# Seven block products for the turned queries and keys, their weight sums on GpSimd, and an earlier first modulation sum

## The reference, cut to what matters

```python
mod = jax.nn.silu(cvec) @ w_mod_l + b_mod_l            # 6 rows of 1024
sh1, sc1, g1, sh2, sc2, g2 = jnp.split(mod, 6, axis=-1)
h = x * (1.0 + sc1) + sh1
qa, ka, va, qb, kb, vb, qc, kc, vc = jnp.split(h @ w_in_l, _in_offsets(), axis=-1)
...
ga, gb, gc = jnp.split(jax.nn.sigmoid(h @ w_gate_l + b_gate_l), N_BRANCH, axis=-1)
y = (ga * (oa @ w_br_l[0]) + gb * (ob @ w_br_l[1]) + gc * (oc @ w_br_l[2])) @ w_o_l
```

## Time and profile before

| | us |
|---|---|
| median of 3 runs | 2136.37 (2136.27 to 2140.67) |
| the profiled execution's own time | 2136.38 |
| its span in the profile | 2134.3 |
| PE busy | 2007.2, 94% |
| DVE busy | 1292.1, 61% |
| POOL busy | 238.2, 11% |

### The profile page before, as it was taken

How to read it: one execution, slowest core, us unless ns; L and a number is a source line. 1 busy time by engine, 2 the same in 40 slices (tenths; PEclk the granted TensorE clock), 3 DMA queues, 4 the chain that set the end, 5 groups by cost and what they waited for, 6 DMA issues and landing times. The chain is left out here.

```text
span 2134.3 us, 25339 instructions
## 1 busy us (share of the span) xinstructions
PE 2007.2 (94%) x9546; PEld 1173.9 (55%) x9546; DVE 1292.1 (61%) x2031; ACT 513.9 (24%) x1007; POOL 238.2 (11%) x250
## 2 busy tenths in 40 slices
PE   7999999999999999699899999999999999979995
PEld 3457766566467754344244676656755676434432
DVE  2747747675456665756444574776744665866664
ACT  2114401143124400122130342003402342002221
POOL 1000020421110000100120002031101000010003
PEclk9999999999999999899999999999999999989998
DMA  7631046411120061689781111552111105238996
GB/s 284 243 118 40 21 143 222 138 55 44 40 82 21 33 279 79 247 341 362 257 278 48 64 41 64 195 185 87 48 57 46 43 21 221 105 133 322 385 350 199
DMA packets 62682, 317.00 MB, mean 149 GB/s; under 512 B 14824, under 2 KB 15280, under 8 KB 34272
## 3 DMA queue, kind: packets, MB, share of 16 engines
q1 hardware_dynamic: 32688, 232.41, 28.9%
q0 software_dynamic: 13136, 53.64, 7.7%
q10 hardware_dynamic: 16736, 29.32, 3.8%
HBM read 286.70 MB, written 27.07 MB: 147 GB/s over the span
## 5 line engine op out<-in xcount | busy, mean ns | idle before, releaser
L1217 PE MATMUL ps<-ring,hT 128*128 128x512 f32 (+1 forms) x960 | 388.4, 560 | 4.0 <-DVE hT L2190 2.0
L1217 PE MATMUL ps<-ring,zT 128*128 128x512 f32 (+2 forms) x992 | 317.5, 600 | 2.0 <-ACT zT L2093 2.0
L1217 PE MATMUL ps<-R,ring 128*128 128x512 f32 (+2 forms) x1024 | 292.3, 437 | 6.3 <-DVE zT L2522 3.5
L1217 PEld LDWEIGHTS ps<-ring,hT 128*128 128x128 f32 x960 | 179.4, 191 | 187.4 <-issue 176.7
L1217 PE MATMUL ps<-hT,ring 128*128 128x320 f32 x896 | 260.5, 436 | 0.0
L1217 PEld LDWEIGHTS ps<-R,ring 128*128 128x128 f32 x1024 | 161.9, 191 | 118.0 <-issue 92.8
L1217 PEld LDWEIGHTS ps<-ring,zT 128*128 128x128 f32 (+2 forms) x992 | 121.5, 156 | 149.0 <-issue 146.4
L1217 PEld LDWEIGHTS ps<-hT,ring 128*128 128x128 f32 x896 | 164.8, 190 | 65.2 <-issue 2.6
L2370 DVE SCALAR_TENSOR_TENSOR R<-ring,cs,R 128x2048 f32<-128x2048 f32 x70 | 173.3, 2476 | 8.3 <-DMA ring<-in_wall 5.5
L2025 ACT COPY R<-ps 128x512 f32<-128x512 f32 (+2 forms) x170 | 96.1, 565 | 271.3 <-PE ps L1506 253.8
L1445 PE MATMUL ps<-R 64*128 64x128 f32 (+2 forms) x992 | 123.2, 374 | 5.7 <-ACT R L1896 2.5
(11 more groups left out here) (335 smaller groups left out, 2460.8 us busy)
## 6 DMA issues: line engine op xcount, KB each, us to landing
ring<-in_wall SPq DMA_DIRECT2D x188, 1024.0 KB, 6.0
hT<-in_wall SPq DMA_DIRECT2D x20, 1024.0 KB, 8.9
y_all<-R ACTq DMA_DIRECT2D x27, 512.0 KB, 6.9
R<-in_wall SPq DMA_DIRECT2D x10, 1024.0 KB, 9.0
R<-in_rows POOLq DMA_DIRECT2D x2, 4096.0 KB, 17.9
R<-mrows POOLq DMA_DIRECT2D x16, 512.0 KB, 21.5
R<-in_x ACTq DMA_DIRECT2D x10, 512.0 KB, 8.9
h_rows<-R ACTq DMA_DIRECT2D x10, 512.0 KB, 2.6
```

The source lines that it names most:

```text
L1217: ins = nc.tensor.matmul(out, w, m, start=start, stop=stop, **kw)
```

## The change

Chunks 3 and 4 are computed as four pairs of column tiles (q = 0 to 3), each by seven products of 4 matmuls of 128x320. GpSimd makes the four sums of weight blocks of a pair (each 128x4x128), for pairs 0 and 1 ahead of its `masked_bias`, for pairs 2 and 3 behind it, each when the pair two before is done. ACT copies two of the seven products, VectorE adds the other five in six operations. The 32 modulation passes of VectorE are interleaved: 7 in merge(0), one behind each tile but the last, 19 between the additions of the pairs, 6 behind them. The first group has its own accumulators; `sum_partials` for it stands behind pair 1. The order of the loads becomes 2 of chunk 3, 4 of the modulation, 2 of chunk 4, 4 of the modulation, 2 of chunk 5, 8 of the modulation.

```diff
-MOD_ORDER = ((2, 6, 0), (0, 0, 8))
-MOD_SUMS = ((4, 1), (5, 3))
+MOD_ORDER = ((4, 4, 0), (0, 0, 8))
+MOD_SUMS = ((3, 3), (5, 3))
+FIRST_SUMMED = 1
+PASSES = ((1, 1, 1, 1, 1), (1, 1, 1, 1, 0), (1, 1, 1, 1, 1), (1, 1, 1, 1, 1))
...
-PROJECT_SLOTS = (0, 1, 2, 3, 4, 5) + 3 * (2, 3) + (0, 1) + 4 * (2, 3)
+PROJECT_SLOTS = (0, 1, 2, 3, 2, 3, 4, 5, 2, 3, 2, 3, 0, 1) + 4 * (2, 3)
...
+TURNED_BANKS = (2, 3, 2, 4, 5, 0, 1)
...
+        first_acc = [area(5632, 2048), area(8704, 2048)]
...
# GpSimd
+                    def sum_turned(q):
+                        for i in turned_pieces(layer, q):
+                            pool.wait_ge(full[slot_of(layer, i)], 16 * loads_by(layer, i))
+                        if q >= 2:
+                            pool.wait_ge(pe_acc, turned_no(q - 2, HIGH_HIGH))
+                        (a11, a12), (a21, a22) = turned_weights(layer, q)
+                        both, cross, far = turned_sums[q % 2]
+                        ch.step(nc.gpsimd.tensor_tensor(both, a21, a22, ALU.add), g_turn)
+                        ch.step(nc.gpsimd.tensor_tensor(cross, both, a11, ALU.subtract), g_turn)
+                        ch.step(nc.gpsimd.tensor_tensor(a21, a11, a21, ALU.subtract), g_turn)
+                        ch.step(nc.gpsimd.tensor_tensor(far, a12, cross, ALU.subtract), g_turn)
...
+                            sum_turned(0)
+                            pool.wait_ge(pe_gate, gate_no(0, PAIRS - 1, LATE))
+                            pool.wait_ge(v_anorm, NT)
+                            sum_turned(1)
                             for g in range(LAT):
                                 masked_bias(0, g)
                             load_bias(1)
+                            for q in range(TILE_PAIRS, TURNED_PAIRS):
+                                sum_turned(q)
...
-                                pool.wait_ge(a_copy, AU.index(PU.index((br, c, units(c) - 1))) + 1)
+                                pool.wait_ge(v_turn, turned_adds(TURNED_PAIRS - 1, HIGH_HIGH))
# TensorE
+                    def turned_pair(q):
...
+                        for o in range(SEVEN):
...
+                            elif o == CROSS:
+                                if q:
+                                    pe.wait_ge(v_turn, turned_adds(q - 1, CROSS))
+                                pe.wait_ge(g_turn, SUMS * q + 2)
+                                weights, tokens = cross, lambda k: token_row(layer, 0, 1, k)
...
+                            for k in range(STEPS):
+                                last = mm(ps[:, TURNED_BANKS[o], 0:320], weights[:, k, :], tokens(k), k == 0 and o != HIGH_LOW, k == STEPS - 1,
+                                          frees=k < STEPS - 1, skip_group_check=o in (LOW_LOW, HIGH_LOW))
+                            last.then_inc(pe_acc, 1)
...
+                            if turned(c):
+                                for q in range(TILE_PAIRS * (c - 3), TILE_PAIRS * (c - 2)):
+                                    turned_pair(q)
+                                    if q == FIRST_SUMMED:
+                                        sum_partials(1 + (layer == 0), first_acc)
+                                used(2)
+                                continue
# VectorE
                         if br == 1:
-                            modulation_partials()
+                            for q in range(TURNED_PAIRS):
+                                for o, n in zip((CROSS, DOWN, ACROSS, LATE, HIGH_HIGH), PASSES[q]):
+                                    add_turned(q, o)
+                                    partials(n)
+                            partials(4 * KB)
                             gate_sums(1, 0)
...
+                    def add_turned(q, o):
+                        dve.wait_ge(pe_acc, turned_no(q, o))
+                        if o == CROSS:
+                            dve.wait_ge(a_copy, AU.index(PU.index((1, 3, 0))) + 2 * q + 1)
+                        got = ps[:, TURNED_BANKS[o], 0:320]
+                        _, second, third_, fourth = turned_quarters(q)
+                        scale = HD ** -0.5 if q < TILE_PAIRS else 1.0
+                        for out, acc, sign in {CROSS: ((fourth, fourth, 1.0),), DOWN: ((third_, fourth, 1.0),),
+                                               ACROSS: ((second, fourth, 1.0), (fourth, third_, 1.0)), LATE: ((second, second, 1.0),),
+                                               HIGH_HIGH: ((third_, third_, -1.0),)}[o]:
+                            ch.step(V_.scalar_tensor_tensor(out, got, sign * scale, acc, ALU.mult, ALU.add), v_turn)
...
                             if br == 0:
                                 ch.step(V_.scalar_tensor_tensor(g, g, 1.0, src, ALU.add, ALU.mult), v_z)
+                                if m < KB - 1:
+                                    partials(1)
```

More of the change, by code:

```diff
@@ L322, in turned @@
     return c in (3, 4)
+TILE_PAIRS = 2
+TURNED_PAIRS = 4
+TURNED_BANKS = (2, 3, 2, 4, 5, 0, 1)
 def units(c):
-    return 8 if turned(c) else NT
+    return 2 * TILE_PAIRS if turned(c) else NT
 def lat(i):
@@ L435, in build_kernel @@
         part_sum = area(26624, 512).rearrange("p (k n) -> p k n", k=4)
+        first_acc = [area(5632, 2048), area(8704, 2048)]
         cross_sum = sb("cross_sum", [128, 4, 128])
+        turned_sums = [[a.rearrange("p (k n) -> p k n", k=4) for a in (area(13824, 512), area(14336, 512), area(17664, 512))],
+                       [cross_sum[:], tmpA.rearrange("p (k n) -> p k n", k=4), tmpB.rearrange("p (k n) -> p k n", k=4)]]
         cexp = area(18176, KB * 32).rearrange("p (k n) -> p k n", k=KB)
@@ L645, in upto, with turned_pieces, pieces_index, turned_weights @@
                         done[0] += 1
+        def turned_pieces(layer, q):
+            return [pieces_index(layer, ("in", 3 + q // TILE_PAIRS, h)) for h in range(2)]
+        def pieces_index(layer, what):
+            return STREAM[layer].index((layer, what))
+        def turned_weights(layer, q):
+            b = 2 * (q % TILE_PAIRS)
+            tiles = [slot_at(slot_of(layer, i)).rearrange("p (k n) -> p k n", k=4) for i in turned_pieces(layer, q)]
+            return [[w[:, :, 128 * m:128 * m + 128] for w in tiles] for m in (b, b + 1)]
+        def turned_quarters(q):
+            b, both = 2 * (q % TILE_PAIRS), (QT, KT)[q // TILE_PAIRS]
+            return (both[:, b, early], both[:, b, late], both[:, b + 1, early], both[:, b + 1, late])
+        def turned_no(q, o):
+            return PU.index((1, 3, 0)) + SEVEN * q + o + 1
+        def turned_adds(q, o):
+            return ADDS * q + (0, 1, 1, 2, 4, 5, 6)[o]
+        def acc_no(i):
+            return i + 1 + (SEVEN * TURNED_PAIRS - 2 * units(3) if PU[i][1] >= 5 and PU[i][0] else 0)
         class Chain:
@@ L1245, in sum_partials @@
                             for j in range(STRIPS):
-                                last = nc.tensor.matmul(ps[32 * j:32 * j + 32, 6, :], unit_col[:, v, :], mod_acc[:, v, 512 * j:512 * j + 512],
+                                last = nc.tensor.matmul(ps[32 * j:32 * j + 32, 6, :], unit_col[:, v, :], acc[v][:, 512 * j:512 * j + 512],
                                                         start=v == 0, stop=v == 1)
@@ L1322, in first_units @@
                         used(1 if h else 1 + KB // 2)
+                    def turned_pair(q):
+                        for h in range(2):
+                            take("in", h)
+                        (a11, a12), (a21, a22) = turned_weights(layer, q)
+                        both, cross, far = turned_sums[q % 2]
+                        copied = AU.index(PU.index((1, 3, 0))) + 2 * q
+                        for o in range(SEVEN):
+                            if o == LOW_LOW:
+                                if q:
+                                    pe.wait_ge(a_copy, copied)
+                                weights, tokens = a11, lambda k: hT[:, k, early]
+                            elif o == CROSS:
+                                if q:
+                                    pe.wait_ge(v_turn, turned_adds(q - 1, CROSS))
+                                pe.wait_ge(g_turn, SUMS * q + 2)
+                                weights, tokens = cross, lambda k: token_row(layer, 0, 1, k)
+                            elif o == HIGH_LOW:
+                                pe.wait_ge(a_copy, copied + 1)
+                                weights, tokens = a12, lambda k: hT[:, 4 + k, early]
+                            elif o == DOWN:
+                                if q:
+                                    pe.wait_ge(v_turn, turned_adds(q - 1, DOWN))
+                                pe.wait_ge(g_turn, SUMS * q + 3)
+                                weights, tokens = a21, lambda k: token_row(layer, 0, 2, k)
+                            elif o == ACROSS:
+                                if q:
+                                    pe.wait_ge(v_turn, turned_adds(q - 1, ACROSS))
+                                weights, tokens = both, lambda k: token_row(layer, 0, 0, k)
```

(51 more changed lines are left out.)

29 lines of the change are left out of this document (16 added, 13 removed).

## The result

| | before | after |
|---|---|---|
| median, us | 2136.27 (2132.72 to 2140.67, 7 runs) | 2143.12 (2142.22 to 2151.01, 7 runs) |
| ratio of the runs | 1 | 1.0041, 95% interval 1.003 to 1.0052 |
| profiled execution, us (span) | 2136.38 (2134.3) | 2151.01 (2149.2) |
| PE busy | 2007.2 | 1999.6 |
| DVE busy | 1292.1 | 1334.0 |

A forecast was written before the change was run, and what follows sets the result against it. It took TensorE, busy 94% of the span, as the bound. Matmuls -17.3, first stalls +9.8, second +5.1 and clock +4.0 gave +1.6 us on 2136.38: 2138.0 us, range 2124 to 2149.

The forecast's parts named there:

- the side that had the smallest chance: Whole kernel: slower than before, chance 0.31, against faster 0.37 and same 0.32.
- The mechanism: At TensorE's two sums: GpSimd's operations and VectorE's passes take turns, VectorE lacks slack, so TensorE waits and can lose clock.
- the signs that it named: Timelines: gaps of about 5 and 1 to 4 us before the sums, passes 3 to 4.9, additions 0.49, half clock.
- the third rival: At both sums: each GpSimd operation costs VectorE its full length; +12.2 us, 2148.6 us; chance 0.27.
- Matmuls, -8.65 a layer: Changed stage on TensorE: 112 matmuls of 128x320 instead of 128, 0.540 us each; -17.3 us for both layers.
- GpSimd's sums: 1.26 each, never waited for: Weight sums of 128x512 on GpSimd: 1.26 us each, ready before TensorE needs them; their cost is VectorE's time.
- Passes in merge(0), nothing: VectorE's seven passes in merge(0): no cost to TensorE, bound 3 us if two tiles are held.
- First wait, 4.9: TensorE before the first sum, both layers: waits 4.9 us for VectorE's passes, between 2.6 and 8.1.
- Second wait, 3.5 and 1.6: TensorE before the second sum: token differences delay VectorE, stalls of 3.5 us in layer 0, 1.6 in layer 1; bounds 0 and 5.2.
- Clock, 2.0 a layer: TensorE behind the first stall loses 2.0 us a layer to reduced clock, behind the second 0; bounds 0 and 4 a layer.
- The first rival: Milder overlap: TensorE waits 2.6 us at the first sums only and keeps its clock; -12.1 us, 2124.3 us; chance 0.26.
- The second rival: All covered: no stall of TensorE anywhere, 2119.1 us; chance 0.05.

The follow-up runs named there:

- e4: Changed kernel with the first sum moved behind DOWN of pair 2 and GpSimd's branch-1 token differences moved behind VectorE's last pass: 2119.9 us, ratio 0.9923 to the kernel before.
- e1: Changed kernel with GpSimd's weight sums for pairs 2 and 3 over 8 columns instead of 512 (wrong results): 2136.84 us, ratio 1.0008 to the kernel before.
- e2: Changed kernel with GpSimd's token differences of branch 1 waiting until VectorE is through all 32 passes: 2132.48 us, ratio 0.9982 to the kernel before.
- e6: Changed kernel with TensorE running throw-away 128x320 matmuls before its waits, 9 at the first sum, 7 at the second: 2140.13 us, ratio 1.001 to the kernel before.
- e3: Changed kernel with TensorE's first sum behind DOWN of pair 2 instead of behind pair 1, ACT's keeping moved too: 2124.33 us, ratio 0.9945 to the kernel before.

## Why the prediction came out as it did

The forecast was 2138.0, no measurable difference; the kernel is 0.41% slower, inside a wide range (2124 to 2149) but on the side that had the smallest chance, 0.31. The mechanism is the forecast's, and of the signs that it named one was off: passes beside sums took 2.7 to 3.1 us, not 3 to 4.9. Of the sizes the first waits are those of the forecast, the second waits those of the third rival (8.0 us in all, where it had 8.3), and the clock's loss is above both. In time the kernel lies 8.8 us above the one before by the ratio: nearer to the rival's 12.2 than to the forecast's 1.6.

- *Matmuls, -8.65 a layer.* Right: 14 products from 302.31 to 332.5, and e4 gives the sum back to 0.1 us.
- *GpSimd's sums: 1.26 each, never waited for.* Right: 1.26 to 1.28 us free, and no gap within a pair.
- *Passes in merge(0), nothing.* Right. The merge of TensorE is again one group of 28.59 us, with passes of 2.5 to 2.8 us.
- *First wait, 4.9.* Measured 5.13 and 5.12: GpSimd's share is 2.2 by e1, where the step said 2.3, and VectorE's own 2.95, where it said 2.6.
- *Second wait, 3.5 and 1.6.* Mis-sized in layer 1: 3.95 and 4.00. There I took the 5.38 us that the store of keys needed in rows 7; here it landed in 2.04 and 2.05 us in the two layers, so the differences started earlier and lengthened the last seven passes by 9.2 us in both layers (25.84 against 16.64), where the step had 9.2 and 7.3. A landing time of one execution was used as if it belonged to the layer. The 2.7 us of a difference of 1280 was also misread: the line through rows 6 and 7 gives 2.88, and the free ones of e2 take 2.87 and 2.90.
- *Clock, 2.0 a layer.* This is the step that failed most. I left the second wait without a loss ("near the border"). Both waits lose: by the trace 1.5 to 1.7 us at each sum, and 0.40 and 0.65 us in the group behind the first (2.82 and 3.07 us, where e6 has 2.42 at full clock). With 0.13 us behind the second sum of layer 1 that is 3.8 in layer 0 and 4.0 in layer 1, my upper bound of 4. e6 removes 3.7 and 3.85.

With measured sizes the sum nearly closes: -17.3 + 10.25 (first waits) + 7.95 (second) + 7.8 (clock) = +8.7, against 9.1 as the difference of the stages. Of the 7.1 us by which the sum exceeds the forecast's +1.6, the clock has 3.8, the second wait 2.85 and the first 0.45.

The first rival (2.6 us of wait, clock kept) is what e1 builds in part, and even there the clock was lost once. The second rival fails by the first wait. The third had the right sign; its mechanism is shown by e1 and e2, but its full price per operation is not reached, because GpSimd slips under additions. The rule of the Trainium skill ("SBUF — State Buffer", section "Who interferes with whom") held both ways: passes and sums excluded each other, additions with one SBUF operand stayed at 0.49 us.

The rule there has a condition that the prediction left out: one SBUF input is free of contention only outside VectorE's 2-port modes, which `tensor_scalar` can enter. The trace after agrees in merge(0): the first pass over a piece reads one SBUF tensor, and a sum that starts beside it still takes 2.16 us, not 1.26 (timeline of VectorE, first fence, and of GpSimd, second fence). No trace here names the mode.

```profile
276.23 1.29 DVE L2492 TENSOR_SCALAR R<-ring,cs 128x2048 f32<-128x2048 f32 x1
```

```profile
276.49 2.16 POOL L1114 TENSOR_TENSOR ring<-ring 128x512 f32<-128x512 f32 x1
```

## What to carry to other kernels

Shortening the bounding engine's work shortens the time that its helpers have: before pricing the saving, sum the helper's work between two of its deadlines, with what a neighbour that excludes it takes from it. A long wait of TensorE can be dearer than its length: in the changed kernel each of the four, 3.95 to 5.13 us, cost 1.65 to 2.4 us again. When such a wait appears, look first for what can be moved behind the deadline (here six differences needed later, and one sum needed by nobody soon): the two moves turned +0.4% into -0.8%.

## What the runs showed of the hardware that I had not expected

How long a gap TensorE can stand without losing its clock was not fixed in these runs. In e1 a gap of 2.95 us was followed by a sum of 3.37 us in layer 0 and of 1.92 in layer 1, in e3 one of 1.97 by 1.92 and one of 1.95 by 3.00; before, one of 2.64 kept the clock (TensorE's timeline, first fence, and the window behind the gap, second fence, columns as in rows 10):

```profile
1065.47 1.98 PE L898 MATMUL ps<-R,ident 128*128 128x512 f32 x4 [2.64 <-DMA R<-y_all,yrow]
```

```profile
1066.00:1069.00 3.00, 3.00 (x8) 1.14 (x6) 0.85 (x4) 1.24 (x1) 0.57 (x1) 1.00 1.03 345
```

From 3.9 us on every gap in these stages lost it. The loss varied: with a wait of 5.13 us in layer 1 of e2 the sum took 3.27 us, 1.35 more than at full clock, and nothing behind it; with one of 4.12 in layer 0 of e1 it took 3.64, and the group behind it 8.29 rather than 7.13, 2.9 us in all. Throw-away matmuls that end 0.3 to 0.4 us ahead of the wait's end kept the clock at full (e6), and VectorE, which was waited for, was not later for them.
